# Third mixer's attention: the scores of the two key groups as a pair on the two halves of TensorE's rows

## The reference, cut to what matters

```python
l_s = einsum('bqgrd,bgqkd->bgrqk', qq, k_s) * scale + bias      # g: 2 groups, r: 4 heads of a group
p_s = softmax(where(m_s, l_s, NEG_INF), axis=-1)
o_s = einsum('bgrqk,bgqkd->bqgrd', p_s, v_s)                    # o_w the same with k_w, v_w
o = gg[..., 0:1] * o_c + gg[..., 1:2] * o_s + gg[..., 2:3] * o_w
```

## Time and profile before

| what | value |
|---|---|
| runs shown | 3762.26, 3765.64, 3765.16 us, median 3765.16 |
| profiled execution | 3762.98 us, its span 3761.1 us |
| PE busy | 3699.8 us, 98% |
| DVE, ACT, POOL busy | 37%, 20%, 28% |
| attention of the third mixer | 3057 to 3166 us of the span |

### The profile page before, as it was taken

How to read it: one execution, slowest core, us unless ns; L and a number is a source line. 1 busy time by engine, 2 the same in 40 slices (tenths; PEclk the granted TensorE clock), 3 DMA queues, 4 the chain that set the end, 5 groups by cost and what they waited for, 6 DMA issues and landing times.

```text
span 3761.1 us, 42034 instructions
## 1 busy us (share of the span) xinstructions
PE 3699.8 (98%) x17561; PEld 2623.7 (70%) x17561; DVE 1379.1 (37%) x2219; ACT 747.7 (20%) x1327; POOL 1045.5 (28%) x919
## 2 busy tenths in 40 slices
PE   8999999999999999999999999999999999999999
PEld 7888667775554788864575444478887557858888
DVE  3221210422111322135635200178822274248851
ACT  2000251223110100012332300010012354230000
POOL 4544100000000355423441000146640020016653
PEclk9999999999999999999999999999999999999999
DMA  4322444333232232232232222233223310023322
GB/s 130 90 79 83 84 66 69 57 62 62 57 67 78 79 90 87 84 96 73 84 100 86 70 75 78 78 84 85 87 91 110 72 42 4 6 59 87 90 84 73
DMA packets 370368, 286.07 MB, mean 76 GB/s; under 512 B 11283, under 2 KB 360083, under 8 KB 370180
## 3 DMA queue, kind: packets, MB, share of 16 engines
q1 hardware_dynamic: 369892, 283.11, 28.6%
q10 hardware_dynamic: 288, 0.27, 0.0%
HBM read 280.64 MB, written 2.72 MB: 75 GB/s over the span
## 4 chain that ended last, share of the span: by engine, by line
PE 96%; DVE 1%; ACT 1%; DMA 1%; issue 1%; POOL 0%; SPq 0%; DVEq 0%; ACTq 0%
PE psum L604 42%; PE psum L1999 14%; PE psum L1319 6%; PE psum L2192 3%; PE psum L1440 3%; PE psum L2890 3%; PE psum L1354 2%; PE psum L1146 2%; PE psum L1116 2%; PE psum L3730 1%; PE psum L1986 1%; PE psum L1112 1%; PE psum L3465 1%; PE psum L573 1%; PE psum L2976 1%; PE psum L2996 1%
## 5 line engine op out<-in xcount | busy, mean ns | idle before, releaser
L604 PE MATMUL psum<-work 128*128 128x256 f32 (+1 forms) x2400 | 551.4, 381 | 0.0
L523 POOL TENSOR_TENSOR work<-weight_ring 128x512 f32<-128x512 f32 x132 | 163.1, 1236 | 1378.5 <-PE psum L604 735.7
L604 PEld LDWEIGHTS psum<-work 128*128 128x128 f32 x2400 | 456.0, 190 | 66.0
L604 PE MATMUL psum<-work,weight_ring 128*128 128x256 f32 (+1 forms) x2080 | 481.8, 381 | 0.0
L604 PE MATMUL psum<-normalized,weight_ring 128*128 128x256 f32 (+1 forms) x2016 | 469.5, 383 | 2.7 <-DVE normalized L724 2.7
L1999 PE MATMUL psum<-normalized,weight_ring 128*128 128x512 f32 x1024 | 450.5, 596 | 0.0
L604 PEld LDWEIGHTS psum<-work,weight_ring 128*128 128x128 f32 x2080 | 395.2, 190 | 57.2
L604 PEld LDWEIGHTS psum<-normalized,weight_ring 128*128 128x128 f32 x2016 | 384.4, 191 | 61.3 <-DVE normalized L724 4.2
L1999 PEld LDWEIGHTS psum<-normalized,weight_ring 128*128 128x128 f32 x1024 | 192.0, 191 | 228.4 <-issue 227.3
L748 DVE TENSOR_TENSOR work<-work,psum 128x512 f32<-128x512 f32 (+1 forms) x100 | 68.6, 686 | 643.3 <-PE psum L604 643.3
L682 ACT ACTIVATE work<-psum 128x256 f32<-128x256 f32 (+1 forms) x100 | 38.5, 385 | 1095.9 <-PE psum L604 1095.9
(11 more groups left out here) (514 smaller groups left out, 4757.1 us busy)
## 6 DMA issues: line engine op xcount, KB each, us to landing
weight_ring<-in_w_in SPq DMA_DIRECT2D x73, 1024.0 KB, 7.9
weight_ring<-in_w_ffn_in SPq DMA_DIRECT2D x88, 512.0 KB, 5.1
weight_ring<-in_ffn_w_up SPq DMA_DIRECT2D x44, 512.0 KB, 4.8
weight_ring<-in_ffn_up SPq DMA_DIRECT2D x44, 512.0 KB, 5.1
weight_ring<-in_w_ffn_out SPq DMA_DIRECT2D x16, 1024.0 KB, 5.2
weight_ring<-in_w_out SPq DMA_DIRECT2D x12, 1024.0 KB, 5.2
work<-decay_sums SPq DMA_DIRECT2D x16, 512.0 KB, 4.1
weight_ring<-in_w_proj_b SPq DMA_DIRECT2D x8, 1024.0 KB, 5.1
```

The source lines that it names most:

```text
L523: own(pool.tensor_tensor(s1, a21, a22, ALU.add))
L604: last = pe.matmul(K.ps[:, self.BANK[m] * T:self.BANK[m] * T + self.H], left(m, p), right(pe, m, p), start=first and p == 0, stop=last_par ...
```

## The change

The order of the units has the branch ahead of the group, so that units s and s+1 (s even) differ in the group alone. PE makes the scores of both in even steps, by the new method `scores_pe`: for each piece of at most 256 key columns two products, each over 64 rows only, group 0 on rows 0 to 63 into bank 0 and group 1 on rows 64 to 127 into bank 1. They wait for `scaled` (s), that is until unit s-1 has been scaled (`lora_read` for s=0). `tail_dve` reads gates, partial sums and outputs with the strides of the new order. DVE's loop, ACT's loop, the transposes and the weighting keep their lines; they take g and br from the same list of units.

```diff
     def units(self):
 
         return [(i, jj, j, g, br) for i in range(NT) for jj in range(2) for j in (2 * jj, 2 * jj + 1)
-                for g in range(NSA_GROUPS) for br in range(2)]
+                for br in range(2) for g in range(NSA_GROUPS)]
...
         for s in range(n + 3):
-            if s < n:
-                i, _, j, g, br = units[s]
-                pe.wait_ge(*(S["scaled"](s - 1) if s > 1 else S["lora_read"](4)))
-                pe.matmul(K.bank(s % 2, (i + 1) * P), A(self.q + j * T + i * P, P), A(self.ks + (2 * g + br) * T, (i + 1) * P),
-                          start=True, stop=True).then_inc(S["scored"].h, 1)
+            if s < n and s % 2 == 0:
+                self.scores_pe(pe, s)
...
+    def scores_pe(self, pe, s):
+
+        K, A, S = self.K, self.A, self.s
+        i, _, j, _, br = self.units()[s]
+        width = (i + 1) * P
+        pe.wait_ge(*(S["scaled"](s) if s else S["lora_read"](4)))
+        for c in range(0, width, HALF_BANK):
+            w = min(HALF_BANK, width - c)
+            for g in range(NSA_GROUPS):
+                last = pe.matmul(K.bank(g, w, P, c), A(self.q + j * T + i * P, P, half(g)),
+                                 A(self.ks + (2 * g + br) * T + c, w, half(g)), start=True, stop=True)
+                if c + w == width:
+                    last.then_inc(S["scored"].h, 1)
...
-        gate = A(self.gates + i * GATE_W, GATE_W).rearrange("p (g j b) -> p j g b", g=NSA_GROUPS, b=3)[:, 2 * jj:2 * jj + 2, :, 1:3]
-        scale4 = scale.rearrange("p (j g b) -> p j g b", g=NSA_GROUPS, b=2)
+        gate = A(self.gates + i * GATE_W, GATE_W).rearrange("p (g j b) -> p j b g", g=NSA_GROUPS, b=3)[:, 2 * jj:2 * jj + 2, 1:3, :]
+        scale4 = scale.rearrange("p (j b g) -> p j b g", g=NSA_GROUPS, b=2)
...
-        parts = out.rearrange("p (x b n) -> p x b n", b=2, n=HEAD)
+        parts = out.rearrange("p (j b n) -> p j b n", j=2, b=2)
...
-        last = dve.tensor_tensor(y, y, out.rearrange("p (j g b n) -> p j g b n", j=2, g=2, b=2)[:, :, :, 0, :], ALU.add)
+        last = dve.tensor_tensor(y, y, out.rearrange("p (j b g n) -> p j b g n", j=2, b=2, g=2)[:, :, 0, :, :], ALU.add)
```

## The result

| kernel | runs | median | lowest to highest |
|---|---|---|---|
| before | 8 | 3764.18 us | 3761.03 to 3767.96 |
| changed | 8 | 3773.56 us | 3770.36 to 3777.82 |

The ratio is 1.0024, 95% interval 1.0016 to 1.0033: slower by 0.24%, some 9 us. Run again beside other kernels the ratio was 1.0026 (1.0017 to 1.0035). The forecast was 3773 with a range of 3760 to 3780.

The account below looks back on a forecast made before the run. TensorE (PE) was taken as the bound, 96% of the chain. Row halves -6.4, look-ahead +6.0+2.5+0.8 (together +2.9) and clock +5.1 gave +8.0 us on the 3765.16 median: 3773, range 3760 to 3780.

Parts of the forecast that it names:

- Part 1: Scores, all 32 pairs: row halves take 1.06, 0.85, 0.63, 0.42 us plus 0.14 behind; gain 6.4 us in all.
- Part 2: Look-ahead: PE's scores wait for both scalings of a pair; holes (A), (B), (C) cost 6.0, 2.5, 0.8 us.
- (A): Step 10 of each i: DVE's tails between a pair's scalings; PE idles 2.10 to 3.05 us, 6.0 us over before.
- (B): Step 2 of i=1, 2, 3: last group's tail on DVE; PE idles 1.0, 0.8, 0.58 us, 2.5 with refill.
- (C): Step 4: compressed scores on DVE; PE idles about 0.16 us at i=3, 2, 1; 0.8 us with refills.
- Part 3: PE's clock behind holes (A) at i=1, 2, 3: three falls, 5.1 us; bounds 0 and 10 us.
- Part 4: The rest (transposes, weightings, tail strides, DMA, POOL): nothing, within 0.1 us for each of 8 groups either way.
- The first: Rival, clock in the attention: it holds, one fall or none; +2.9 to +4.6 us, about 3769; chance 0.18.
- The bare pair: Rival, the 32 pairs: they stream without the 0.34 us charge; 3763.7, or 3758.5 with the clock holding; chance 0.15.
- The third rival: Holes (B) and (C) also lower the clock, or half-clock stretches join; +13 to +16 us, about 3779; chance 0.15.

Follow-up runs that it names:

- run 7: Changed kernel with full-height products for the pairs and DVE's three side jobs one step later: 3761.39 us, ratio 0.9995 to the kernel before.
- run 12: run 8 with two unused products on PE before unit 14 at i=0: 3753.72 us, ratio 0.9979 to the kernel before.
- run 2: Kernel before with only the new unit order and the tail's new strides; scores and look-ahead as before: 3761.72 us, ratio 1.0000.
- run 3: Changed kernel with full-height products for the pair's scores, its wait kept: 3775.11 us, ratio 1.0029 to the kernel before.
- run 11: run 4 with one more unused product in each of two idle stretches at the start of i=0: 3763.30 us, ratio 1.0004.
- run 1: Changed kernel with DVE's three side jobs (compressed scores, compressed tail, group tail) one step later: 3757.72 us, ratio 0.9986 to the kernel before.
- run 6: Kernel before with DVE's three side jobs one step later: 3761.78 us, ratio 0.9995.
- run 4: Changed kernel with two unused 0.86 us products ahead of PE's wait at step 12 of each tile: 3766.47 us, ratio 1.0009 to the kernel before.
- run 9: Changed kernel with i=0 scored full-height, one unit at a time, with the old look-ahead; side jobs not moved: 3766.74 us, ratio 1.0011.
- run 10: run 8 with score pieces of up to 512 columns in place of 256: 3755.23 us, ratio 0.9981 to the kernel before.
- run 8: run 1 with i=0 scored full-height, one unit at a time, with the old look-ahead: 3754.08 us, ratio 0.9972 to the kernel before.
- run 5: Changed kernel once more, unedited: 3772.68 us, ratio 1.0026 to the kernel before.

## Why the prediction came out

- **Part 1, the row halves.** The pairs and the 0.14 behind them were right to 0.01 us. From the end of the hole at step 12 of i=0 to the end of the attention run 7 takes 92.5 us and run 12 84.1; some 1.6 of the difference is the clock that run 7 lost, going by before and run 2, which leaves 6.8 for i=1 to 3 where the sum had 7.4. The loss of 1.0 at i=0 was not seen: from the first scores to the end of that hole the full-height pairs of run 3 take 14.1 us and the row halves of run 11 14.4, with 0.3 of it for the unused product. The stretch ends in a wait for DVE in both, so PE is not the bound there.
- **Part 2, the look-ahead.** The mechanism was right: the order of DVE's stream puts the jobs between the scalings of a pair, and run 1 undoes just this. The holes were 3.05, 2.7, 2.4, 2.1 (A) and 1.0, 0.8, 0.6 (B) in the prediction and 2.73, 2.62, 2.41, 2.08 and 0.64, 0.66, 0.58 in the trace. (C) had three small ones and the trace has one of 0.21: the margin was 0.16 us in 2.96, within the error of the terms. At (B) of i=1 DVE's hold was as predicted, 3.03 us from the end of the pair (3085.76 less 3082.73), but PE reached the wait 0.3 us later than the sum had it. Parts 1 and 2 together were to be +2.9. Run 2 (the kernel before but for the order) and run 11 (the changed kernel with its idle stretches filled) both keep the clock up, and show parts 1 and 2 without part 3:

| tile | run 2 | run 11 | more | the prediction's parts 1 and 2 |
|---|---|---|---|---|
| i=0 | 16.3 | 17.5 | +1.2 | +1.6 |
| i=1 | 21.0 | 23.3 | +2.4 | +1.9 |
| i=2 | 28.5 | 29.0 | +0.5 | +0.6 |
| i=3 | 40.2 | 38.8 | -1.4 | -1.2 |
| all | 105.9 | 108.6 | +2.8 | +2.9 |

  These two parts were right in sum, and by tile to 0.5 us; 0.3 of run 11's time at i=0 is its unused product.
- **Part 3, the clock.** This term failed, in size and in place: 5.1 us in the prediction. The trace has 10.2 us of extra lost clock, and 7.0 of it became time (8.6 between the changed kernel and run 11, less 1.6 between the kernel before and run 2). The prediction took every fall as one stretch of 1.7 and looked for falls only behind the new holes. The trace has one it had no place for, at the start of i=0 (3.4); those behind step 12 of i=0 and i=1 are twice as long (3.4 each); and the hole of 2.08 us at i=3, which it counted, did not lower the clock, though 1.93 in run 3, 1.78 in run 1 and 2.14 before did. Nor does a hole of over 2 us always lower it: 2.35 in run 3, 2.29 in run 2 and 2.26 in run 6 did not. 3.4+(3.4-1.7)+3.4+1.7=10.2. Runs 4 and 11 show that it is the clock: with the idle stretches filled by useless work, the time drops by 5 and then by all of the loss.
- **Part 4** was right within what run 2 can show, 0.1% either way.
- **The sum.** +8.0 was forecast and +9.4 measured; on the chain the attention has 2.8 for parts 1 and 2 and 7.0 for the clock, where the prediction had 2.9 and 5.1. That the number came out within 1 us is in part luck: the base of the forecast, the median of three runs, was 1.0 above that of eight, and in the clock's term a fall that nobody foresaw and two of twice the length stand against one that was foreseen and did not come. The first table by tile shows it, where only i=2 agrees.
- **The rivals.** The first needed one fall or none; the clock held behind one new hole of three. The bare pair is excluded by the chain. The third rival's longer stretches did come, at i=0 and i=1, with less effect than the 5 us that it priced (7.0 became time where the forecast had 5.1), for i=3 stayed clean.

Open is what decides whether the clock falls behind a hole, and why it stays at half for 3.4 us behind some holes and 6.8 behind others. The hole at step 12 of i=0 is 2.26 to 2.29 us in six kernels with single full-height scores there, and by their profiled executions it cost no clock in two (runs 2 and 6), 1.7 us in three (before, runs 9 and 10) and 3.4 in one (run 8). So neither the length of the hole nor the shape of the products before it settles this, and one execution does not give the pattern of a kernel. That the changed kernel's long stretches come from its row halves is not shown. Open is also whether any of the 1.4 us outside the attention is the change's.

## What to carry to other kernels

When two products are joined so that they run side by side, the wait in front of them becomes the later of two: look at the consumer's stream for anything that stands between its two parts, and move it behind the second before judging the joined products (here a shift of three jobs by one step turned 9 us of loss into 4 of gain, and 10 with the thin tile left alone). Price a hole in PE's stream twice, as idle time and as clock, and check in the profile of the new kernel both where the clock fell and for how long. To see the two apart, compare kernels in which the clock stayed up, rather than taking the lost clock off the length. A forecast that comes out on the number should still be checked term by term.

## What was not expected of the hardware

- Useless products on PE made the kernel faster: 1.7 us of them in each of four holes took the ratio from 1.0026 to 1.0009, and with two more at the start to 1.0004.
- At the start of i=0 the granted clock stayed 1.00 with full-height products (before, runs 2, 3, 6, 7, 8, 9, 10, 12) and fell with row halves (changed, runs 1, 4, 5), for 3.4 us of lost clock or more, with no idle stretch over 0.92 us. It stayed up with row halves too once the idle stretches were filled (run 11). In run 3 the stretches before the first two pairs are 0.89 and 0.52 us, in the changed kernel 0.92 and 0.71; whether the row halves or these 0.2 us of idle make the difference is not shown.
- The pattern of falls repeated itself exactly between two profiled executions of the changed kernel (2.41 us fell, 2.08 did not), though they began 2.3 us apart in their spans; the hole of 2.26 to 2.29 us at i=0 of the full-height kernels had three different outcomes in six.
- Of the clock lost, a part never became time: 3.4 us lost made the attention 2.4 us longer in run 8 than in run 12.
- Two 64-row products of 512 columns overlap as well as pieces of 256: 1.06 us per pair either way, 0.20 above one full-height product.
